# Three of the six copies of transposed queries and keys in units 6 to 11, made by ScalarE in place of VectorE

## What is computed

```python
def second_block(x, ...):
    for l in range(DEPTH_2):                        # 2 layers
        x = _layer_norm(alpha * x + 0.5 * _swiglu(x, ...), ...)
        mix = _token_mixers(x, w_in[l], ...)        # here
        x = _layer_norm(alpha * x + mix, ...)
        x = _layer_norm(alpha * x + 0.5 * _swiglu(x, ...), ...)

def _token_mixers(h, ...):
    proj = h @ w_in
    a, b, c, d = jnp.split(proj, ...)
    o_a = _mixer_window(a, sink, slopes)    # 4 heads of 64, bias, a sink logit
    o_b = _mixer_mla(b, ...)                # 4 heads of 96, queries and keys rotated
    o_c = _mixer_axial(c, ...)              # 4 heads of 64
    o_d = _mixer_diff(d, ...)               # 4 heads, two softmax maps of 32 each, bias
    return jnp.concatenate([o_a, o_b, o_c, o_d], axis=-1) @ w_out
```

## Time and profile before

| | us |
|---|---|
| median of 3 runs | 1750.41 |
| lowest, highest | 1749.85, 1752.44 |
| time of the profiled execution | 1750.45 |
| its span, first to last instruction | 1748.7 |
| TensorE busy in the span | 1609.7 (92%) |
| VectorE busy | 957.6 (55%) |
| ScalarE busy | 622.5 (36%) |
| GpSimd busy | 226.6 (13%) |

### The profile page before, as it was taken

How to read it: one execution, slowest core, us unless ns; L and a number is a source line. 1 busy time by engine, 2 the same in 40 slices (tenths; PEclk the granted TensorE clock), 3 DMA queues, 4 the chain that set the end, 5 groups by cost and what they waited for, 6 DMA issues and landing times.

```text
span 1748.7 us, 27045 instructions
## 1 busy us (share of the span) xinstructions
PE 1609.7 (92%) x10486; PEld 1219.6 (70%) x10497; DVE 957.6 (55%) x1493; ACT 622.5 (36%) x961; POOL 226.6 (13%) x241
## 2 busy tenths in 40 slices
PE   8999999777777776999999999999999999999998
PEld 6788985333323332788887788888888887788886
DVE  5675543111111110677776767677767766677767
ACT  5464431100010000443443643444344443653332
POOL 0232110000000000100133321001110133411000
PEclk9999999888767877999999999999999999999999
DMA  9515489999999999955445055533854534055511
GB/s 396 195 63 169 172 338 386 426 426 427 424 427 426 425 426 427 369 213 190 175 176 193 1 222 199 180 108 133 330 181 168 216 127 186 25 220 191 195 43 49
DMA packets 61100, 421.47 MB, mean 241 GB/s; under 512 B 7024, under 2 KB 16080, under 8 KB 17360
## 3 DMA queue, kind: packets, MB, share of 16 engines
q1 hardware_dynamic: 59280, 409.13, 59.7%
q10 hardware_dynamic: 1728, 11.03, 1.7%
HBM read 419.08 MB, written 1.05 MB: 240 GB/s over the span
## 4 chain that ended last, share of the span: by engine, by line
PE 64%; DMA 11%; SPq 9%; DVE 6%; issue 4%; POOL 3%; ACT 2%; DVEq 0%; ACTq 0%; POOLq 0%
PE bank L1162 17%; PE bank L1205 12%; DMA ring<-in_we 9%; SPq L2047 9%; PE bank L1164 9%; PE bank L2198 6%; PE bank L2224 2%; PE bank L2127 2%; PE bank L683 2%; PE bank L1545 2%; POOL x L1056 2%; DMA ring<-in_wf 2%; PE bank L1192 1%; PE bank L1183 1%; PE bank L1151 1%
## 5 line engine op out<-in xcount | busy, mean ns | idle before, releaser
L1162 PE MATMUL bank<-xhl,whu 128*128 128x512 f32 x1280 | 451.8, 396 | 0.0
L1164 PE MATMUL bank<-xhl,wlu 128*128 128x256 f32 x1280 | 357.5, 279 | 0.0
L1162 PEld LDWEIGHTS bank<-xhl,whu 128*128 128x128 f32 x1280 | 240.3, 188 | 57.8
L1164 PEld LDWEIGHTS bank<-xhl,wlu 128*128 128x128 f32 x1280 | 241.1, 188 | 3.3
L979 DVE TENSOR_TENSOR wlu<-ring,whu 128x2048 fp32r<-128x2048 f32 x84 | 192.5, 2292 | 43.9 <-ACT whu L974 43.9
L974 ACT ACTIVATE whu<-ring 128x2048 fp32r (+1 forms) x88 | 167.2, 1902 | 3.5 <-DMA ring<-in_wf 3.5
L979 DVE TENSOR_TENSOR wld<-ring,whd 128x1024 fp32r<-128x1024 f32 x80 | 98.6, 1233 | 113.4 <-ACT whd L974 113.4
L683 PE MATMUL bank<-ring,xg 128*32 128x256 f32 x1424 | 115.0, 466 | 39.1 <-DMA ring<-in_we 39.1
L974 ACT ACTIVATE whd<-ring 128x1024 fp32r (+1 forms) x80 | 84.8, 1060 | 128.5 <-PE bank L1205 128.5
L1272 ACT ACTIVATE sg<-sg 128x256 f32<-128x256 f32 x80 | 33.5, 418 | 265.8 <-DVE sg L1351 265.8
L683 PEld LDWEIGHTS bank<-ring,xg 128*32 128x32 f32 x1424 | 46.2, 126 | 99.4 <-DMA ring<-in_we 68.1
(11 more groups left out here) (349 smaller groups left out, 2777.4 us busy)
## 6 DMA issues: line engine op xcount, KB each, us to landing
ring<-in_we SPq DMA_DIRECT2D x141, 1024.0 KB, 26.9
ring<-in_wf SPq DMA_DIRECT2D x88, 1536.0 KB, 6.4
ring<-in_w SPq DMA_DIRECT2D x52, 1024.0 KB, 5.0
more<-in_we SPq DMA_DIRECT2D x51, 1024.0 KB, 25.8
ring<-in_w SPq DMA_DIRECT2D x32, 256.0 KB, 3.7
ln<-in_ln ACTq DMA_DIRECT2D x6, 1024.0 KB, 5.9
bias<-in_bias ACTq DMA_DIRECT2D x2, 2048.0 KB, 7.3
bias<-in_bias SPq DMA_DIRECT2D x1, 2048.0 KB, 20.4
```

Source lines behind the costliest of these rows:

```text
L1162: pe.matmul(into[:].rearrange("p (a s) -> p a s", a=2), whu[p][:, cols], xhl[:, :, k], start=(k == 0), stop=False, skip_group_check=True)
L1164: ins = pe.matmul(into[:, 0:S], wlu[p][:, cols], xh[:, k], start=False, stop=(k == KD - 1), skip_group_check=True)
```

## The change

ScalarE's `between` gets the copies of turns 6, 9 and 11, behind its copy of the transposed probabilities of the same turn. VectorE keeps those of turns 7, 8 and 10. The three have scale 1.0, so that a plain copy does. Banks, destinations and semaphore counts stay as they were, and so does TensorE's list.

```diff
@@ act_layers, between(u)
                         act.activation(qm[:, i].rearrange("p h d -> p (h d)"), bank[7 - i][:, 0:BH * BQ], ACT.Copy)\
                            .then_inc(c_a, 1)
+                    if u == 6:
+                        act.wait_ge(t_ps, tb + 10)
+                        act.activation(qkT2[:, block2(6):block2(6) + 2].rearrange("p k s -> p (k s)"), bank[7][:], ACT.Copy)\
+                           .then_inc(t_out, 1)
+                    if u in (9, 11):
+                        j = u - 8
+                        act.wait_ge(t_ps, tb + (12 + j))
+                        at_b = block2(13 + j)
+                        act.activation(qkT2[0:BQ, at_b:at_b + 2, :], bank[6][0:BQ].rearrange("p (b s) -> p b s", b=2), ACT.Copy)\
+                           .then_inc(t_out, 1)
@@ dve_layers, between(u)
-                    if u == 6:
-                        group(3, 7)
                     if u == 7:
                         group(4, 6, scale=64 ** -0.5)
-                    if 8 <= u < 12:
+                    if u in (8, 10):
                         j = u - 8
                         dve.wait_ge(t_ps, tb + (12 + j))
-                        at_b = block2(10 + 4 * (j % 2) + 2 * (j // 2))
-                        dve.tensor_scalar(qkT2[0:BQ, at_b:at_b + 2, :],
-                                          bank[7 - j % 2][0:BQ].rearrange("p (b s) -> p b s", b=2),
-                                          (BQ ** -0.5, 1.0)[j % 2], None, ALU.mult).then_inc(t_out, 1)
+                        at_b = block2(10 + j)
+                        dve.tensor_scalar(qkT2[0:BQ, at_b:at_b + 2, :], bank[7][0:BQ].rearrange("p (b s) -> p b s", b=2),
+                                          BQ ** -0.5, None, ALU.mult).then_inc(t_out, 1)
```

## The result

The changed kernel takes 1767.97 us (median of 6 runs, 1758.82 to 1770.11) against 1751.50 for the kernel before in the same session (6 runs, 1749.85 to 1755.32). Its time comes out 1.008 times that of before, with a 95% interval of 1.0057 to 1.0103. The medians lie 16.5 us apart. I had forecast 4.5, so the sign was right and the size was not: the range ended at 1756.6.

The account below looks back on a forecast made before the run. TensorE was taken as the bound, 92% busy, waiting on its helpers' queues. Per layer 1.35 + 0.38 + 0.50 = 2.23, twice 4.46, on 1750.41 gave 1754.9 us (chance 0.76), range 1752.0 to 1756.6.

Parts of the forecast that it names:

- The wait of turn 6: TensorE's scores of units 8 and 9 wait for ScalarE's later copy: 1.35 us later per layer.
- Turns 9 and 11: Copies delay ScalarE's exponentials of units 10 and 12, for which TensorE waits: 0.38 and 0.50 us per layer.
- the sum: Waits of turns 6, 9 and 11 added: 2.23 us per layer, 4.46 for two layers.
- VectorE gives nothing back: VectorE's 0.59 us won in turn 6 is lost again waiting for scores; in turn 11 it wins nothing.
- Nothing absorbs the delay: Work behind the units starts from TensorE, without slack; the rival that the delay is absorbed, 1750.4 us, had 0.06.
- the clock stayed at 1.00 through the waits in the earlier trace: Argument against TensorE's 1.35 us hole lowering the granted clock to 1.2 GHz.
- the rival of the greater loss: Copies don't overlap on ScalarE, 1755.5 us, or TensorE's hole lowers the clock, 1759.5 us; chance 0.07.
- The signs: Timeline marks: 1.3 us idle ahead of units 8 and 9's scores, exponentials at 1.00, later probabilities, VectorE less busy.

Follow-up runs that it names:

- e1_fill: The changed kernel plus six TensorE products of zeros ahead of the wait for turn 6's copy, copies and waits kept; 1761.26 us, against 1750.88 before.
- g1_fill_all: e1_fill plus products of zeros ahead of the values of units 7, 9, 11 and the probabilities of units 10, 12; 1754.66 us, against 1751.17 before.
- a1_again: The changed kernel itself run once more, unchanged; median 1766.52 us, against 1751.72 for the kernel before.
- f1_dve_thrice: The kernel before with turn 6's copy made three times on VectorE, no copy on ScalarE; 1762.10 us, against 1750.88 before.
- b1_turn6: The changed kernel with only turn 6's copy on ScalarE, those of turns 9 and 11 back on VectorE; 1769.73 us, against 1751.72 before.
- f2_dve_twice: The kernel before with turn 6's copy made twice on VectorE, no copy on ScalarE; 1753.84 us, against 1750.88 before.

## Why the prediction was wrong, point by point

- **The wait of turn 6: right, slightly too large.** Forecast 1.35, measured 1.24. I had taken 0.14 from the end of ScalarE's copy to TensorE's product; here it is 975.19 + 0.59 = 975.78 to 975.83, 0.05. The copy itself came 0.01 sooner and was 0.01 shorter.
- **Turns 9 and 11: right.** Forecast 0.38 and 0.50; from L2427 to the exponentials it is 0.97 where it was 0.62 and 0.50, so 0.35 and 0.47. Together the waits come to 2.09 a layer (e1_fill, layer 2) against 2.23 in the sum. g1_fill_all, the change with its clock held up, lies 3.5 over before by its median; the forecast for the waits was 4.46.
- **VectorE gives nothing back: right.** Its logits of unit 8 wait 1.89 instead of 0.42.
- **Nothing absorbs the delay: right.** The 17.3 us of the ruler in a1_again are the 17.1 of the whole execution.
- **The step that failed: "the clock stayed at 1.00 through the waits in the earlier trace rows", under the rival of the greater loss.** By this the sum put the clock at nothing. It was true of before, but the longest wait of TensorE in the stretch of the earlier trace rows is 0.78; the 0.99 of the earlier trace rows lies outside it, at 1005.33. I carried it over to a hole longer than both. I named the mechanism and even its place, gave it 0.07, and priced it at two microseconds of slow products a layer. Measured, it is between 3.4 and 20 us of slow products, 1.5 to 8.0 us lost in a layer, in both profiles of the change. The missing term was the largest of all: 12 of 16.5 us.
- **The shape of the result.** I gave one number for runs that spread over 11 us. A term that depends on whether and when the clock falls makes such a spread, and the range should have been open at that end: it stopped at 1756.6, short of the 1759.5 that I had worked out myself for a fall of the clock. That 1759.5 is close to the two runs near 1759 is partly luck, for nothing showed how long a fall lasts.
- **The signs.** What I had named as signs of being right came true: 1.17 of idle time ahead of L2350, released by L1727, 0.97 to the exponentials, the probabilities of unit 10 taken up 1.57 later (forecast 1.73) and those of unit 12 2.05 later (forecast 2.23), counted from the transposes of unit 6's. None of them looks at the granted clock, so they could not tell the forecast from the greater loss.

What stays open is why the clock falls right behind turn 6 in one execution, behind turn 11 in another, and in one layer of f1_dve_thrice not at all. The wait ahead of the scores of units 8 and 9 is the same to 0.01 us each time in one kernel (1.17 or 1.18, and 1.33 in f1_dve_thrice), so something that these rows don't show decides it. The page TensorE: Matmul & The Clock Gate of the Trainium skill, section Part 1: The HAM clock gate, says that the chip watches activity in windows that run freely and don't start with the kernel; that would fit, and no run here could set the phase to test it.

## What to carry to other kernels

A helper's work costs what its place in the helper's list costs: the same three copies are free ahead of a copy that waits for TensorE anyway, and 16 us behind it. Before an instruction is moved, look up who waits for its semaphore and how soon, and put it into the idle time that ends ahead of that. When a wait makes TensorE stand idle longer than any wait in that part does now, do not price it at its length: the granted clock can fall and stay down for many times that, in some runs and not in others. Whether it is the clock can be tested by filling the hole with useless products.

## What the runs showed of the hardware

- One idle stretch of TensorE of 1.17 us, in a part in which it is otherwise busy some nine tenths of the time, took the clock from 2.4 to 1.2 GHz in both layers of b1_turn6, and it stayed there for some 20 us although TensorE worked all the while at half speed (0.87 and 0.85 over 80 and 70 us). It need not happen each time: no fall followed directly on the 1.17 in the first profile of the change, nor on the 1.33 in layer 1 of f1_dve_thrice. Single waits of 0.60 (f2_dve_twice) and 0.99 (before) went without a fall in their profiles.
- The clock that was not granted came to 1.7, 6.8, 8.5 or 10.2 us in a layer. Most of it shows in the time: 1.5 of 1.7 (the profile of the result), 5.7 of 6.8 (e1_fill), 8.3 of 10.2 (b1_turn6). A part of the rest is idle time that TensorE has at full speed and not while it is slow: the two waits of 0.34 for ScalarE ahead of the values of units 7 and 9 are missing from b1_turn6's slow stretch.
- A ScalarE copy of 512 fp32 columns out of PSUM held its list up for 0.47 to 0.49 us, with 96 partitions as with 128; the same copy on VectorE 0.59 to 0.60.
